# Eleven slots for U rows, five for V rows, and V rows asked for half a head later, in a two-layer hybrid decoder with PEER experts

## The reference, cut to what matters

```
qry = x @ wq; sc = qry . sub_keys        # 8 heads, two halves of 128 scores
top 16 of each half, top 16 of the 256 sums -> 16 expert rows eidx, weights g
a = gelu(einsum('td,tkd->tk', x, expert_u[eidx]))     # dot products with U rows
y = einsum('tk,tkd->td', a * g, expert_v[eidx])       # weighted sum of V rows
e = sigmoid(x @ ple_wg + ple_bg) * (p[i] @ ple_wp)    # per-layer embedding
x = layer_norm(alpha * x + y + e)
```

## Time and profile before

| | us |
|---|---|
| median of 3 runs | 3516.88 (3516.3 to 3517.65) |
| the profiled execution | 3518.44 |
| its span, first to last instruction | 3516.7 |
| PE matmuls busy | 2765.0 (79%) |
| DVE busy | 2369.1 (67%) |
| POOL busy | 1981.9 (56%) |
| ACT busy | 615.2 (17%) |
| bytes moved by DMA | 1164.86 MB, of them 1073.87 MB gathered rows |

### The profile page before, as it was taken

How to read it: one execution, slowest core, us unless ns; L and a number is a source line. 1 busy time by engine, 2 the same in 40 slices (tenths; PEclk the granted TensorE clock), 3 DMA queues, 4 the chain that set the end, 5 groups by cost and what they waited for, 6 DMA issues and landing times.

```text
span 3516.7 us, 23931 instructions
## 1 busy us (share of the span) xinstructions
PE 2765.0 (79%) x6672; PEld 1221.2 (35%) x6672; DVE 2369.1 (67%) x5146; ACT 615.2 (17%) x1468; POOL 1981.9 (56%) x2100
## 2 busy tenths in 40 slices
PE   8999888766667877766699998887666678787666
PEld 4655443222223323222246554433222233232222
DVE  1435777777777777886514347777777778778864
ACT  1231221111111211111113312211110111111111
POOL 0001366777676767777500014667776767677774
PEclk9989999988889989888899899998888899898898
DMA  4112799999999999999831137999999999999998
GB/s 146 66 48 100 278 404 407 409 409 409 407 409 394 408 408 398 404 408 402 311 138 48 48 116 283 404 407 409 409 409 407 409 393 402 406 402 408 404 408 311
DMA packets 351321, 1164.86 MB, mean 331 GB/s; under 512 B 36690, under 2 KB 66514, under 8 KB 350932
## 3 DMA queue, kind: packets, MB, share of 16 engines
q0 software_dynamic: 294912, 1073.87, 77.2%
q1 hardware_dynamic: 53812, 89.15, 7.2%
q10 hardware_dynamic: 2464, 0.31, 0.1%
HBM read 1161.10 MB, written 2.10 MB: 331 GB/s over the span
## 4 chain that ended last, share of the span: by engine, by line
PE 37%; DMA 27%; POOL 13%; DVE 13%; issue 6%; ACT 3%; DVEq 0%; ACTq 0%; SPq 0%; POOLq 0%
DMA arena<-in_peer_u,rows 15%; DMA arena<-in_peer_v,rows 11%; PE bank L1514 10%; POOL arena L546 7%; POOL arena L537 7%; DVE arena L1011 6%; PE bank L1333 5%; PE yv L1306 5%; PE bank L1306 4%; PE bank L1488 3%; PE yv L1462 2%; DVE yv L1040 2%; ACT arena L740 2%; PE yv L1375 1%; PE bank L1312 1%
## 5 line engine op out<-in xcount | busy, mean ns | idle before, releaser
L1514 PE MATMUL bank<-arena 128*128 128x512 f32 x3072 | 1674.4, 694 | 687.5 <-DMA arena<-in_peer_v,rows 518.8
L1011 DVE CUSTOM_DVE_ANT_0 arena<-arena,xps 128x1024 f32<-128x1024 f32 x1024 | 1240.7, 1215 | 426.7 <-DMA arena<-in_peer_u,rows 398.3
L537 POOL DMA_INDIRECT arena<-in_peer_u,rows x1024 | 973.8, 951 | 566.3 <-issue 254.6
L1514 PEld LDWEIGHTS bank<-arena 128*128 128x128 f32 x3072 | 634.9, 219 | 1718.7 <-DMA arena<-in_peer_v,rows 919.6
L546 POOL DMA_INDIRECT arena<-in_peer_v,rows x1024 | 970.6, 948 | 395.9 <-issue 260.4
L1040 DVE SCALAR_TENSOR_TENSOR yv<-arena,yv 128x1024 f32<-128x1024 f32 x248 | 317.9, 1282 | 46.6 <-DMA arena<-in_peer_v,rows 38.1
L579 ACT ACTIVATE arena<-arena 128x16 f32<-128x16 f32 x64 | 13.9, 218 | 1883.8 <-DVE arena L1011 1883.6
L740 ACT ACTIVATE arena<-keep,arena 128x128 f32<-128x128 f32 x768 | 231.3, 387 | 103.4 <-DVE arena L1027 102.8
L1333 PE MATMUL bank<-xT,arena 128*128 128x128 f32 (+2 forms) x768 | 228.5, 457 | 4.4 <-ACTq L712 3.1
L1306 PE MATMUL yv<-arena,xT 128*128 128x512 f32 (+1 forms) x384 | 167.1, 590 | 0.0
L1306 PE MATMUL bank<-arena,xT 128*128 128x512 f32 (+1 forms) x384 | 161.7, 578 | 4.2 <-DMA arena<-in_w_in 4.2
(11 more groups left out here) (287 smaller groups left out, 1955.8 us busy)
## 6 DMA issues: line engine op xcount, KB each, us to landing
arena<-in_w_in SPq DMA_DIRECT2D x12, 2048.0 KB, 8.8
arena<-in_peer_wq SPq DMA_DIRECT2D x24, 1024.0 KB, 9.6
arena<-in_peer_u,rows POOLq DMA_INDIRECT x1024, 11.1
arena<-in_peer_v,rows POOLq DMA_INDIRECT x1024, 11.2
arena<-in_w_out SPq DMA_DIRECT2D x4, 2048.0 KB, 7.8
arena<-in_ple_wg SPq DMA_DIRECT2D x4, 2048.0 KB, 20.9
arena<-in_mixer SPq DMA_DIRECT2D x2, 2112.0 KB, 19.7
ln<-in_ln SPq DMA_DIRECT2D x8, 512.0 KB, 8.0
```

Of the source, the lines that this page charges most:

```text
L537: e.indirect_dma_start(urow[i % UR], None, a["peer_u"], bass.IndirectOffsetOnAxis(ap=rows[:, n % RR, k:k + 1], axis=0)).then_inc(u_in[i % ...
L1011: e.tensor_tensor_reduce(r, r, xps[:, :], 1.0, 0.0, ALU.mult, ALU.add, dots[:, n % 2, k:k + 1]).then_inc(u_free, 1)
L1514: ins = e.matmul(bank[m][:, :], diag[:, k, :], vrow[i % VR][:, m * 512:(m + 1) * 512], start=(h == 0 and k == 0), stop=(h == PH - 1 and k ...
```

## The change

The rings become eleven slots for U rows and five for V rows. V rows fill words 0 to 5119 of the arena. The three slots up to word 8192 (`spare`, `early`) become U slots 8 to 10, and as they lie in the mixer's weight buffers POOL now waits for the last output projection before U(0,8). V rows are asked for `LAG` = 8 rows later: beside U(n+1,k) POOL now asks for V row 16n + k - 8, so V(n,0) comes beside U(n+1,8) and V(n-1,14) beside U(n+1,6). DVE adds its V rows 8 dot products later. The sum of a block is added to `acc` after dot product 9 of the block's second head (n = 9, 17, 25) and no longer after the 16 of its first. The counts of the landing semaphores follow the new ring sizes (`fetched`). Nothing in ACT's program is changed, nor in PE's but for slot numbers and counts.

```
-UR, VR, DR, KR, VD = 8, 8, TOPK, 4, 4
+UR, VR, DR, KR, VD, LAG = 11, 5, TOPK, 4, 4, 8
...
+        spare = 2 * WB // D - VR
+        early = take(spare * D).rearrange("p (s d) -> p s d", s=spare)
+        uring = take((UR - spare) * D).rearrange("p (s d) -> p s d", s=UR - spare)
+        urow = [uring[:, s, :] for s in range(UR - spare)] + [early[:, s, :] for s in range(spare)]
...
+        def fetched(l, i, ring):
+            return 16 * (l * len(range(i % ring, ROWS, ring)) + i // ring + 1)
...
                 for k in range(TOPK):
+                    if k == UR - spare:
+                        e.wait_ge(*step_done("out", 2 * NB - 1))
                     gather_u(0, k)
-                e.wait_ge(*step_done("out", 2 * NB - 1))
                 for n in range(PAIRS):
                     if n + 1 < PAIRS:
                         e.wait_ge(chosen_rows, n + 2)
                     for k in range(TOPK):
                         if n + 1 < PAIRS:
                             gather_u(n + 1, k)
-                        gather_v(n, k)
+                        if n * TOPK + k >= LAG:
+                            gather_v(n * TOPK + k - LAG)
+                for i in range(ROWS - LAG, ROWS):
+                    gather_v(i)
...
-                        if n > 0 and on_vector(k):
-                            add_row(n - 1, k, i + 1)
+                        if on_vector(k) and i >= TOPK + LAG:
+                            add_row((i - TOPK - LAG) // TOPK, (k + LAG) % TOPK, i + 1)
+                        if n % PH == 1 and n > PH and k == LAG + 1:
+                            add_y(n // PH - 1)
...
-                    if n % PH == 0 and n > 0:
-                        add_y(n // PH - 1)
                     if n in PLE_AT:
                         add_ple(PLE_AT[n])
...
-                for k in range(VD - 1, TOPK, VD):
-                    add_row(PAIRS - 1, k)
+                for i in range(ROWS - TOPK - LAG + VD - 1, ROWS, VD):
+                    add_row(*divmod(i, TOPK))
```

More of the change, by code:

```diff
@@ L92 @@
 PAIRS = NB * PH
+ROWS = PAIRS * TOPK
 SPANS = {0: (0, P), 1: (P, SEQ), 2: (0, SEQ)}
@@ L267, in build @@
         vrow = [vring[:, s, :] for s in range(VR)]
-        uring = take(UR * D).rearrange("p (s d) -> p s d", s=UR)
-        urow = [uring[:, s, :] for s in range(UR)]
+        spare = 2 * WB // D - VR
+        early = take(spare * D).rearrange("p (s d) -> p s d", s=spare)
+        uring = take((UR - spare) * D).rearrange("p (s d) -> p s d", s=UR - spare)
+        urow = [uring[:, s, :] for s in range(UR - spare)] + [early[:, s, :] for s in range(spare)]
         wq_all = take(2 * KT * QD)
@@ L536, in gather_u, with gather_v @@
                         e.wait_ge(u_free, i - UR + 1)
-                    e.indirect_dma_start(urow[i % UR], None, a["peer_u"], bass.IndirectOffsetOnAxis(ap=rows[:, n % RR, k:k + 1], axis=0)).then_inc(u_in[i % UR], 16)
-                def gather_v(n, k):
-                    i = n * TOPK + k
+                    slot = i % UR
+                    e.indirect_dma_start(urow[slot], None, a["peer_u"], bass.IndirectOffsetOnAxis(ap=rows[:, n % RR, k:k + 1], axis=0)).then_inc(u_in[slot], 16)
+                def gather_v(i):
+                    n, k = divmod(i, TOPK)
                     if i >= VR and on_vector(i - VR):
@@ L545, in gather_v @@
                         e.wait_ge(v_free, tensor_rows(i - VR) + 1)
-                    e.indirect_dma_start(vrow[i % VR], None, a["peer_v"], bass.IndirectOffsetOnAxis(ap=rows[:, n % RR, k:k + 1], axis=0)).then_inc(v_in[i % VR], 16)
+                    slot = i % VR
+                    e.indirect_dma_start(vrow[slot], None, a["peer_v"], bass.IndirectOffsetOnAxis(ap=rows[:, n % RR, k:k + 1], axis=0)).then_inc(v_in[slot], 16)
                 e.wait_ge(chosen_rows, 1)
                 for k in range(TOPK):
+                    if k == UR - spare:
+                        e.wait_ge(*step_done("out", 2 * NB - 1))
                     gather_u(0, k)
-                e.wait_ge(*step_done("out", 2 * NB - 1))
                 for n in range(PAIRS):
@@ L1008, in dot_products @@
                         i = n * TOPK + k
-                        e.wait_ge(u_in[i % UR], (l * (PAIRS * TOPK // UR) + i // UR + 1) * 16)
-                        r = urow[i % UR]
+                        slot = i % UR
+                        e.wait_ge(u_in[slot], fetched(l, i, UR))
+                        r = urow[slot]
                         e.tensor_tensor_reduce(r, r, xps[:, :], 1.0, 0.0, ALU.mult, ALU.add, dots[:, n % 2, k:k + 1]).then_inc(u_free, 1)
@@ L1032, in add_row @@
                     i = n * TOPK + k
-                    e.wait_ge(v_in[i % VR], (l * (PAIRS * TOPK // VR) + i // VR + 1) * 16)
+                    slot = i % VR
+                    e.wait_ge(v_in[slot], fetched(l, i, VR))
                     w = wgt[:, n % 2, k:k + 1]
                     if n % PH == 0 and k == VD - 1:
-                        e.tensor_scalar(yv[:, :], vrow[i % VR], w, None, ALU.mult).then_inc(v_added, 1)
+                        e.tensor_scalar(yv[:, :], vrow[slot], w, None, ALU.mult).then_inc(v_added, 1)
                     else:
@@ L1039, in add_row @@
                             e.wait_ge(u_free, dot)
-                        e.scalar_tensor_tensor(yv[:, :], vrow[i % VR], w, yv[:, :], ALU.mult, ALU.add).then_inc(v_added, 1)
+                        e.scalar_tensor_tensor(yv[:, :], vrow[slot], w, yv[:, :], ALU.mult, ALU.add).then_inc(v_added, 1)
                 for step, i in MIXER_STEPS:
@@ L1513, in _ @@
                         for m in range(2):
-                            ins = e.matmul(bank[m][:, :], diag[:, k, :], vrow[i % VR][:, m * 512:(m + 1) * 512], start=(h == 0 and k == 0), stop=(h == PH - 1 and k == TOPK - 2))
+                            ins = e.matmul(bank[m][:, :], diag[:, k, :], vrow[slot][:, m * 512:(m + 1) * 512], start=(h == 0 and k == 0), stop=(h == PH - 1 and k == TOPK - 2))
                         ins.then_inc(v_free, 1)
```

## The result

The changed kernel takes 4147.6 us (median of 5 runs, 4146.04 to 4152.49); the kernel before took 3517.65 us beside it (5 runs, 3516.3 to 3520.13). The ratio is 1.1792, with a 95% interval of 1.1779 to 1.1805: slower by 630 us. The forecast was 4036 us, slower by 518, with a range up to 4120. The direction and the mechanism came as forecast. The size did not: the time lies 27.6 us above the range, and the forecast held 82% of the loss. What failed is the sum: the landing time after a restart was 6.5 us and not 5.3, `add_y` cost some 20 us and not nothing, and heads 0 to 5 and the end of a layer were 43 us short.

What follows compares the result with a forecast made beforehand. DMA at 409 GB/s was taken as the bound, with POOL close behind. Slow heads and the layer's end summed to 259 us per layer, 518 for two, added to 3518.4 us for 4036 us; range 3925 to 4120.

Steps and rivals of the forecast that it cites:

- What bounds the kernel: Between the mixers DMA's flat 409 GB/s ceiling binds; POOL, at 421 GB/s, is close behind and its long stops lose time.
- The step that moves: PE finishes V(n-1,14) 19.4 us after T, when head n's dot products are done, delaying ACT, DVE and then POOL.
- The sum: Losses over all slow heads and the layer's end: 259 us per layer, 518 for two layers, giving 4036 us.
- `add_y` at nothing: Adding a block's sum between dot products costs nothing either way, at worst 2 us three times.
- Layer norms and copies of x: Per layer, heads 26 to 28 lose 43 us; the first heads of blocks 1 and 2 lose 21 us.
- Heads 0 to 2: Start of each layer: head 1 loses 4 us and head 2, where score copies precede the GELU, 14 us.
- Query heads: Heads 3 to 5: PE's 12.5 us query step makes POOL stop 4.4 us; 6 us lost for all three.
- End of a layer: After the last GELU, V(31,14) is done at T + 35.5 instead of 27.8 us: 8 us more per layer.
- Only U slots matter: Rival: DVE's row V(n-1,11) is in time and eleven U slots cover DVE's absence; 3705 us, 7 in 100.
- The low clock in full: Rival: idle PE drops to its low clock, slowing V rows and projections; 4120 to 4186 us, 9 in 100.
- DMA gains: Rival: the deeper U ring lets DMA run at POOL's 1.245 us per row; 3446 us, 3 in 100.
- Hides completely: Rival: ACT's late work meets only idle time, so heads keep DMA's 41 us and nothing changes; 1 in 100.

## What the prediction had right, and which of its terms failed

**What bounds the kernel: right.** Plain heads stay at 41 to 42 us and 409 GB/s, and the loss lies in stops of POOL.

**The step that moves: right, and shown.** V(n-1,14) is done at T + 20.0 (the embedding step's start) where 19.4 was forecast, and the edits that cut the two paths behind it take 155.5 us of span (the diagonals, 4150.7 to 3995.2) and 326.5 (the embedding step, to 3668.7) out of the 634; the lag of four rows moves it by the 10 us that POOL's list says.

**The sum: 116 us too small.** This is the step that failed. Its working was right for head 17 but for three small pieces: 0.6 us in R, 0.2 in the step to the restart, 1.4 from the restart to T(18). If each of the 16 embedding heads lost these 2.2 us, they come to some 35 us, an estimate. The largest piece is the landing time, and the prediction had named it as its least sure. It was read in the last rows of the kernel before, eight V rows behind a stop of POOL. After a restart the landing time climbs from row to row: in head 17 V(17,0) lands 4.0 us after its issue, the next row after 5.0, the fifth after 6.5, and U(18,15), the fourteenth row, after 6.5. Issue to landing of line 555 from the restart in head 17 to its end (1267.5:1292), of line 545 at U(18,15) alone (1283.5:1284), and of line 555 in plain heads at 900:1000 us:

```profile
DMA to landing us min/median/max: 4.0/6.6/6.7
...
DMA to landing us min/median/max: 6.5/6.5/6.5
...
DMA to landing us min/median/max: 8.2/9.6/16.9
```

DVE could have been the limit in its place, as the bounds allowed. In head 17 it was not, but only just: of the 24.26 us from the restart to the GELU it is busy for 22.48, and of its dot products there only the last two wait for a row, 0.25 and 1.04 us:

```profile
1290.39 1.22 DVE L1025 CUSTOM_DVE_ANT_0 arena<-arena,xps 128x1024 f32<-128x1024 f32 x1 [1.04 <-DMA arena<-in_peer_u,rows]
```

The bounds had 5.8 as the upper end of the landing, which is 14 us for the whole; 6.5 in its place gives 34 (28 heads times 1.2). The Trainium skill's rule (DMA: Bandwidth & Descriptors, section Anatomy of one DMA — SWDGE (gpsimd) path), by which the landing would be an estimated 3.2 us and the time 3977, is off in the other direction; no gather row in any trace of this case landed in less than 3.9 us.

**`add_y` at nothing: wrong.** Two dot products earlier give 21 us back. This is the one step whose reasoning failed, not only its number: the step was checked for what it waits for, not for what waits for it, and "at worst 2 us three times" had only the first in it.

**Layer norms and copies of x:** the same sum with the same small shortfall, 10 and 12 us in all; 4 us of each come from the mean of 42.1 us, as these heads lasted 41.4 and 41.2 us before. In head 26 DVE is back at T + 27.2 and not 25.0, since the last diagonal ends at T + 22.1; from there to the dot product are 5.2 us, as forecast:

```profile
1789.47 0.40 ACT L753 ACTIVATE arena<-keep,arena 128x128 f32<-128x128 f32 x1 [1.32 <-PE bank L1530]
...
1795.06 1.22 DVE L1025 CUSTOM_DVE_ANT_0 arena<-arena,xps 128x1024 f32<-128x1024 f32 x1
```

**Heads 0 to 2: 18 us short, and the loss lies one head earlier than forecast.** T(1) is 473.6 (forecast 472.8), but the GELU of head 2 comes at 533.0 and not 505. Its dot products were done at 510.3: ACT copies scores ahead of the GELU of head 2, so the wait that was charged to head 2 delays its own GELU and so counts in head 1 (59.4 us), and head 2 is short (36.1). That accounts for the place, not for the 18 us, whose cause was not tested. POOL's stops there:

```profile
445.84 0.94 POOL L555 DMA_INDIRECT arena<-in_peer_v,rows  x1 [6.76 <-DVE yv L1053]
...
483.07 0.94 POOL L555 DMA_INDIRECT arena<-in_peer_v,rows  x1 [17.66 <-DVE yv L1057]
...
541.77 0.94 POOL L555 DMA_INDIRECT arena<-in_peer_v,rows  x1 [18.38 <-DVE yv L1057]
```

**Query heads:** POOL stops 8.3, 7.7 and 6.1 us in layer 0, not 4.4. Twelve us short in all. **End of a layer:** the last V product ends 39.4 us after the GELU (2060.88 + 1.98, GELU at 2023.41), not 35.5; before it was 27.8. Why these two are off was not tested by a run of their own, so 24 of the 116 us stay open besides the 18 above.

```profile
2060.88 1.98 PE L1530 MATMUL bank<-arena 128*128 128x512 f32 x4 [0.16 <-DMA arena<-in_peer_v,rows]
```

**The rivals.** *Only U slots matter* (3705 us) fell: V(n-1,11) was not in time, 38 waits of up to 26.6 us show it. *The low clock in full* had the interval in which the result lies, 4120 to 4186, and is still wrong as a cause: the embedding step takes 7.03 us as before, and the mixer's projections take less than before (325.8 us for line 1321 against 328.8). The low clock is there, 0.50 in the 7.6 us after the restart with one V row at 3.78 us, and PE is busy 100 us longer in all, but these rows are not on the path to the next GELU, which hangs on U(n+1,15). *DMA gains* fell: plain heads (9 to 11) last 41 to 42 us with every ring that was run. *Hides completely* fell.

**The range** was too narrow on its upper side. It let the errors of the terms cancel. But most terms of the sum used the same shallow landing and the same T + 19.4, and they erred to the same side: of the six stretches with a forecast all six came out too small. One bound does not come out of the rows: the -48 us for the extra loads; 1.1 us (42.1 less 41.0) in 28 heads are 31.

## What to carry to other kernels

When a request is moved back in an in-order queue, list what is written behind its consumer on every other engine, before asking whether the buffers are deep enough: here one V row's delay came back through a diagonal's slot and through a matrix step that does not use that row. For a step that is moved, check both what it waits for and who waits for it (`add_y`). And an edit of order is worth only what it is in the present order: the copies behind the GELU saved 21 us with the lag and cost 15 without.

## What the runs showed of the hardware

- The landing time of a 512 KB gather has no single value after a stop of POOL. In the changed kernel's head 17, with one request per 1.24 us, it is 4.0 us for the first row, 5.0 for the second, 6.5 for the fifth and then 6.5 to 6.8. In the last eight rows of the kernel before it goes from 4.1 to 5.8 us. Why it climbs was not tested; requests at 421 GB/s against 409 GB/s moved would fill a queue, but only by 0.035 us per row.
- A deep queue buys no rate here. The plain head above runs at 409 GB/s and in such heads rows land 9.6 us after their issue; before it was the same rate with 17.5 us. By 9.6 / 1.28, an estimate, some 7 or 8 rows in flight are enough for the full rate.
- PE at a granted clock of 0.50, the lower of its two levels (1.2 GHz), after 22.50 us of idle time, took 5.49 us for 6 matmuls in head 16, where the earlier trace rows have 0.50 us each. The embedding step of head 17 ran at a granted clock of 1.00 and took 7.03 us, as before.
